# Two-layer hybrid diffusion step on one Trainium2 core: sixteen modulation tiles move from layer 0's value stage to its input stage

## The reference, cut to what matters

```python
m = jax.nn.silu(cvec) @ w_mod + b_mod          # per layer: 6 rows of 1024, for c_ctx and for c
...
hp = adaln(xp, g_norm2[layer], mp[:, 3], mp[:, 4])
xp = xp + mp[:, 5][:, None, :] * peer(hp, peer_wq[layer], peer_subkeys[layer], peer_u[layer], peer_v[layer])
...
# peer, for each block of 128 tokens
q = (xb @ wq).reshape(tb, PEER_HEADS, 2, PEER_DK // 2)
sc = jnp.einsum('thsd,hskd->thsk', q, subkeys)          # 8 heads x 2 x 128 keys
# top 16 of each half, top 16 of their 256 sums: 128 experts of 16384 for each token
act = jax.nn.gelu(jnp.einsum('td,thkd->thk', xb, u_tab[idx]))
out = jnp.einsum('thk,thkd->td', (gsm * act), v_tab[idx])
```

## Time and profile before

| | |
|---|---|
| median of 3 runs | 4231.42 us (4229.95 to 4235.04) |
| profiled execution, its own time | 4233.31 us |
| its span, first to last instruction | 4231.5 us |
| mean granted clock of TensorE | 0.984 |
| busy: PE / DVE / POOL / ACT | 4083.5 / 2841.0 / 2218.1 / 1221.0 us |
| layer 0's input stage, end of its last matmul | 1395.46 us |
| layer 0's value stage, its first matmul | 1397.98 us |

### The profile page before, as it was taken

The page is one execution under the profiler, slowest core; times in us unless marked ns, Lnnn a source line. Parts: engine busy times, 40 slices in busy tenths (PEclk is TensorE's granted clock), DMA queues, the critical chain, the costliest instruction groups (busy, mean ns, idle before and its releaser), DMA issues.

```text
span 4231.5 us, 57020 instructions
## 1 busy us (share of the span) xinstructions
PE 4083.5 (97%) x19676; PEld 3440.7 (81%) x19676; DVE 2841.0 (67%) x5039; ACT 1221.0 (29%) x1744; POOL 2218.1 (52%) x1784
## 2 busy tenths in 40 slices
PE   7988999999999999999898889999999999999998
PEld 6768988888888788888796689888888888888886
DVE  7877896998125897878634448969981116666665
ACT  2332012232322232333233420122322223333332
POOL 3324447777777554445331134477777755444441
PEclk9989999999999999999999999999999999999999
DMA  5743223333345998888514512333333339888883
GB/s 206 274 175 105 66 107 130 127 129 127 129 143 192 362 350 315 313 313 312 184 54 146 219 65 66 107 130 127 127 129 127 129 120 343 294 290 290 290 287 135
DMA packets 336774, 796.94 MB, mean 188 GB/s; under 512 B 71424, under 2 KB 73184, under 8 KB 336128
## 3 DMA queue, kind: packets, MB, share of 16 engines
q1 hardware_dynamic: 175248, 500.38, 33.4%
q10 hardware_dynamic: 83568, 159.94, 10.2%
q0 software_dynamic: 77824, 134.97, 9.7%
HBM read 640.67 MB, written 154.42 MB: 188 GB/s over the span
## 4 chain that ended last, share of the span: by engine, by line
PE 91%; DVE 5%; DMA 1%; ACT 1%; issue 1%; SPq 0%; POOL 0%; DVEq 0%; ACTq 0%; POOLq 0%
PE acc L605 15%; PE acc L607 15%; PE acc L606 15%; PE aux L887 5%; PE acc L889 5%; PE acc L888 5%; PE aux L888 5%; PE acc L887 5%; PE aux L889 5%; PE acc L842 3%; PE acc L844 3%; PE acc L843 3%; PE aux L812 1%; PE aux L770 1%; DVE unread L1472 1%
## 5 line engine op out<-in xcount | busy, mean ns | idle before, releaser
L574 POOL DMA_INDIRECT gate_d<-gate_v,spot_i x1024 | 1140.3, 1114 | 371.1 <-issue 341.8
L605 PE MATMUL acc<-a_hi,w_hi 128*128 128x512 f32 (+1 forms) x3248 | 1182.8, 364 | 35.0 <-DVE a_lo L1445 30.6
L606 PE MATMUL acc<-a_lo,w_hi 128*128 128x512 f32 (+1 forms) x3248 | 1171.2, 361 | 0.0
L607 PE MATMUL acc<-a_hi,w_lo 128*128 128x512 f32 (+1 forms) x3248 | 1171.1, 361 | 0.0
L605 PEld LDWEIGHTS acc<-a_hi,w_hi 128*128 128x128 f32 x3248 | 613.9, 189 | 130.0 <-issue 48.2
L606 PEld LDWEIGHTS acc<-a_lo,w_hi 128*128 128x128 f32 x3248 | 613.8, 189 | 80.9 <-issue 1.0
L607 PEld LDWEIGHTS acc<-a_hi,w_lo 128*128 128x128 f32 x3248 | 613.2, 189 | 80.1
L1680 DVE TENSOR_TENSOR w_lo<-w_in,w_hi 128x1024 fp32r<-128x1024 f32 x224 | 273.1, 1229 | 573.3 <-ACT w_hi L1213 569.9
L541 POOL DMA_INDIRECT found<-in_v,where_i x256 | 321.1, 1254 | 510.6 <-DVE total L1867 415.1
L1846 DVE TENSOR_TENSOR w_lo<-w_in,w_hi 128x1024 fp32r<-128x1024 f32 x256 | 312.8, 1223 | 223.5 <-ACT w_hi L1252 221.4
L522 POOL CAST w_hi<-w_in 128x1024 fp32r<-128x1024 f32 (+1 forms) x89 | 98.9, 1111 | 664.1 <-DMA w_in<-in_wq 228.4
(11 more groups left out here) (275 smaller groups left out, 5991.4 us busy)
## 6 DMA issues: line engine op xcount, KB each, us to landing
w_in<-in_u SPq DMA_DIRECT2D x256, 512.0 KB, 5.1
w_in<-in_v SPq DMA_DIRECT2D x256, 512.0 KB, 4.9
gate_d<-zeros ACTq DMA_DIRECT2D x32, 2048.0 KB, 7.5
act_s<-l_out ACTq DMA_DIRECT2D x256, 256.0 KB
ag<-act_s SPq DMA_DIRECT2D x256, 256.0 KB, 4.8
ag<-gate_d SPq DMA_DIRECT2D x256, 256.0 KB, 5.7
w_in<-in_in SPq DMA_DIRECT2D x32, 512.0 KB, 7.7
w_in<-in_wq SPq DMA_DIRECT2D x32, 512.0 KB, 3.5
```

Source lines behind the costliest of these rows:

```text
L574: pool.indirect_dma_start(gate_d[l], bass.IndirectOffsetOnAxis(ap=spot_i[:, n, k:k + 1], axis=0), gate_v[:, n, k:k + 1], None).then_inc(sp ...
L605: pe.matmul(out, wh, hi[:, k, n], start=(k == 0), stop=False)
L606: pe.matmul(out, wh, lo[:, k, n], start=False, stop=False)
L607: return pe.matmul(out, wl, hi[:, k, n], start=False, stop=(k == kt - 1))
```

## The change

`MODS_U` goes from 16 to 32 and `MODS_AT` from 112 to 88. Layer 0's input stage then has 40 tiles instead of 24, one beside each of the chunks 88 to 127, and none behind them. The value stage has 16 tiles instead of 32, one in each body, in one buffer instead of two: ahead of chunk 6 in the first body, of chunk 4 in the others. SyncE's part of the input stage is written out for 40 chunks instead of 16, with its wait for `shifted` ahead of chunk 88 instead of chunk 112.

```diff
@@ -276,8 +276,8 @@
         block = ctx.enter_context(nc.Block())
 
         N_CONST, N_CONST1 = 10, 5
-        MODS_U = 16
-        MODS_AT = 14 * SPLIT
+        MODS_U = 32
+        MODS_AT = 11 * SPLIT
         MODS_LATE = 8
         MODS_B, MODS_D, MODS_C = range(16, 26), range(26, 32), range(32, 40)
         B_BESIDE, D_BESIDE = (1, 7), (8, 9, 11, 12, 14, 16)
@@ -459,9 +459,8 @@
                         load_modulation(t)
                     for c in range(MODS_AT, NKEY):
                         load_inputs(c // SPLIT, c % SPLIT)
-                        load_modulation(c - MODS_AT + 4)
-                    for t in range(NKEY - MODS_AT + 4, MODS_LATE + MODS_U):
-                        load_modulation(t)
+                        if c - MODS_AT + 4 < MODS_LATE + MODS_U:
+                            load_modulation(c - MODS_AT + 4)
 
                 def load_values(c, u):
                     slot = u
@@ -490,18 +489,17 @@
                     sp.wait_ge(a_st[s], 16 * A_ALL[s] * (l + 1))
                 for u in range(GROUP, SPLIT):
                     load_ag(u, u)
-                    if l == 0 and u < GROUP + 2:
-                        sp.dma_start(w_mod_v[u - GROUP][:], a["w_mod"][1, MODS_U + u - GROUP])\
-                          .then_inc(mod_v_in[u - GROUP], 16)
+                    if l == 0 and u == GROUP:
+                        sp.dma_start(w_mod_v[0][:], a["w_mod"][1, MODS_U]).then_inc(mod_v_in[0], 16)
                 with sp.Fori(1, BODIES) as i:
                     for u in range(SPLIT):
                         load_ag(u + SPLIT * i, u)
                         sp.wait_ge(v_done, NKEY * l - SPLIT + u + 1 + SPLIT * i)
                         load_values(u + SPLIT * i, u)
-                        if l == 0 and u in (0, 4):
-                            sp.wait_ge(mod_v_used, 2 * i + u // 4 - 1)
-                            sp.dma_start(w_mod_v[u // 4][:], a["w_mod"][1, bass.ds(MODS_U + u // 4 + 2 * i, 1)]
-                                         .rearrange("o p n -> (o p) n")).then_inc(mod_v_in[u // 4], 16)
+                        if l == 0 and u == 0:
+                            sp.wait_ge(mod_v_used, i)
+                            sp.dma_start(w_mod_v[0][:], a["w_mod"][1, bass.ds(MODS_U + i, 1)]
+                                         .rearrange("o p n -> (o p) n")).then_inc(mod_v_in[0], 16)
             for k in range(KD):
                 sp.wait_ge(y_ready, k + 1)
                 sp.dma_start(a["y"][:, k, :], y[:, k, :]).then_inc(y_out, 16)
@@ -1802,8 +1800,6 @@
                         modulate_u(c - MODS_AT)
                     low_u(l, c)
                 if l == 0:
-                    for t in range(NKEY - MODS_AT, MODS_LATE + MODS_U):
-                        modulate_u(t)
                     dve.wait_ge(mod_u_used, MODS_LATE + MODS_U)
                     add_bias(0, 40, 48)
                 step(dve.scalar_tensor_tensor(where[:, 0, :], picks[:, 1, 0, :], float(P), picks[:, 0, 0, :],
@@ -1827,17 +1823,16 @@
                     dve.tensor_tensor(p_los[:, k, :], ag[:, k % 4, 0, :], p_his[:, k, :].bitcast(F), ALU.subtract)\
                        .then_inc(p_lo, 1)
 
-                def modulate_v(i, s):
-
-                    dve.wait_ge(mod_v_in[s], 16 + 16 * i)
+                def modulate_v(i):
+
+                    dve.wait_ge(mod_v_in[0], 16 + 16 * i)
                     for c in range(2):
-                        wait(dve, mod_v_sum, 2 * s + c + 4 * i)
-                        dve.tensor_tensor_reduce(out=unread_v[:], in0=w_mod_v[s][:], in1=c_all[:, c, :], scale=1.0,
+                        wait(dve, mod_v_sum, c + 2 * i)
+                        dve.tensor_tensor_reduce(out=unread_v[:], in0=w_mod_v[0][:], in1=c_all[:, c, :], scale=1.0,
                                                  scalar=0.0, op0=ALU.mult, op1=ALU.add,
-                                                 accum_out=mod_v[:, s, c:c + 1]).then_inc(mod_v_sum, 1)
-                    dve.wait_ge(mod_v_sum, 2 * s + 2 + 4 * i)
-                    dve.tensor_copy(mod[:, 1, bass.ds(MODS_U + s + 2 * i, 1), :], mod_v[:, s:s + 1, :])\
-                       .then_inc(mod_v_used, 1)
+                                                 accum_out=mod_v[:, 0, c:c + 1]).then_inc(mod_v_sum, 1)
+                    dve.wait_ge(mod_v_sum, 2 + 2 * i)
+                    dve.tensor_copy(mod[:, 1, bass.ds(MODS_U + i, 1), :], mod_v[:, 0:1, :]).then_inc(mod_v_used, 1)
 
                 def low_v(i, u):
 
@@ -1870,8 +1865,8 @@
                 def chunk(i, u, q=None, half=0, first=False):
 
                     form(i, u)
-                    if l == 0 and u in ((6, 7) if isinstance(i, int) and i == 0 else (3, 7)):
-                        modulate_v(i, 1 if u == 7 else 0)
+                    if l == 0 and u == (6 if isinstance(i, int) and i == 0 else 4):
+                        modulate_v(i)
                     if q is not None:
                         if u % 4 == 0:
                             parts(q, half)
```

## The result

The changed kernel has a median of 4241.8 us (4236.38 to 4248.04, 12 runs) against 4231.94 for the kernel before on the same chips (12 runs). The ratio is 1.0023, 95% interval 1.0015 to 1.0031: slower by 9.9 us, between 6.3 and 13.1. The forecast was 4237.3 with a range of 4228.5 to 4246, and its likeliest class was "within 0.2%"; the result is in the range, and just beyond the 8.5 us that were to part "slower" from "same"; its interval lies on both sides of that line. The profiled execution took 4239.78 us, its span 4238.0.

The account below looks back on a forecast made before the run. TensorE was taken to bound the kernel, with 91% of the chain that ended last. First wait 8.4, clock 2.0 and second wait 0, less 2.52 and 2.02, gave +5.9 us on 4231.42: 4237.3 us, range 4228.5 to 4246.

Parts of the forecast that it names:

- Sixteen tiles out of the value stage: Value stage: 36.50 us of DVE work leaves, all under a full PE, so 0 us gained.
- Eight tiles from the end of the input stage: Seam to the value stage: 18.3 us of DVE work goes, shortening PE's two waits; 3.0 us gained at best.
- Chunks 88 to 127 without a wait of PE: Input stage: 24 more chunks with a tile leave PE without waits; SyncE's wait for shifted has 86 us to spare.
- The scatters: POOL, layer 0's input stage: tiles stretch gate scatters to 1.618 us each; the last ends at about 1393.6, 26.5 us later.
- The price of a tile: POOL's scatters beside DVE's tiles: each tile costs 1.07 us, not all of its 2.28.
- The third rival: Input stage: tiles block POOL for their whole 2.28 us, scatters run to 1421.8, time 4265.5 us; chance 0.02.
- From the last scatter to PE: Seam: landing 2.0, act_s issue 0.5, gate half of ag 5.7, chain to PE 2.1 us; first value matmul at 1403.9.
- The landing of 2.0 us: Seam: the last scatter takes 2.0 us to land before SyncE goes on, within 1.35 to 7.8.
- The clock: Seam: after its 8.4 us wait PE restarts at a lower clock, losing 2.0 us, between 0 and 2.5.
- The second wait: PE at chunk 4 of the value stage: the old wait of 2.02 us for w_lo falls to 0.
- Three marks that were to show a right forecast: Profile after: last scatter issued between 1388 and 1398, first p_los wait 5 to 11 us, no w_lo wait at chunk 4.
- the slower rival: Seam: landing 7.8 and ag 7.5 us beside POOL's row fetches, first value matmul 1411.5, time 4244.9 us; chance 0.28.

Follow-up runs that it names:

- e5: Kernel before with only the changed kernel's value stage, input stage as before, the 16 tiles between left out; 0.9994 of the kernel before.
- e4: Kernel before with its 24 input-stage tiles beside chunks 104 to 127 and none behind, value stage keeping 32 tiles; 0.9993 of the kernel before.
- e9: Changed kernel with each tile's two products replaced by two sums over the weights alone, one input instead of two; 0.9995 of the kernel before.
- e6: Changed kernel with POOL's first eight row fetches of layer 0 issued behind the first eight pick_act; 1.0022 of the kernel before.
- e8: Changed kernel with a third product of 128 x 1024, result unused, in each of the input stage's 40 tiles; 1.0053 of the kernel before.

## Why the prediction was right, and where it was not, point by point

*Sixteen tiles out of the value stage, 0 us:* right, by PE's 655.00 us of 655.00, and in time, by e5, within 0.15%.

*Eight tiles from the end of the input stage, 3.0 us at best:* right at the seam. e4, which takes the eight from the end and nothing from the value stage, has a first wait of 1.51 and no second one. In time it is 0.9993, not told from 1. In the changed kernel the gain isn't there to be had.

*Chunks 88 to 127 without a wait of PE, and SyncE's wait for shifted hidden:* right; PE's waits have no row between 640 us and the seam.

*The scatters:* the mechanism was right, and so was the pitch with tiles, 1.618 us forecast and 163.40/101 = 1.618 measured, 170.6 scatters forecast by 1371.3 and 169 measured. That the pitch agrees to the last digit is luck: POOL stands idle now and then, which the profile puts down to "issue", and the stretch of the earlier trace rows with tiles has 4.21 us of that in it, the first stretch here 3.10, the second none. Counted without, the pitch was 1.56 before and is 1.59 and 1.62 now. What was mis-sized is the rest: 16.4 scatters in 22.3 us forecast, 19 in 30.1 us measured (1371.3 to 1401.38). An idle stretch of 4.44 us, ahead of 1381.30, fell there. It did not fall there by chance: in layer 0 of every trace 128 scatters lie between one such stretch and the next, and where all 512 are there the last stretch stands ahead of the last 15. So the trace of before could have told where it would be. The last scatter came at 1401.4 and not at 1393.6.

*The price of a tile:* 1.07 us was near enough, but the prediction took it for less than a full block. Each hold is a full one, of one scatter by one operation (e9's rows). The third rival, 2.28 us a tile, failed because every second product finds POOL at work on a scatter that has already been held.

*From the last scatter to PE, 10.3 us:* measured 6.88. The landing of 2.0 us was right (SyncE goes on 1.41 us after the last issue, POOL 2.02). The gate half of ag lands within 2.95 us of its issue, not 5.7: little else was under way (DMA share 0.22 from 1400 to 1405), and the median that I took is over all ag loads, most of them in the value stage's busy DMA (0.83). By luck this error, 3.4 us, goes against that of the scatters, 7.8 us: first value matmul at 1408.26 instead of 1403.9, with inputs that ended 1.25 us later, a first wait of 11.55 instead of 8.4.

*The clock, 2.0 us:* from 1408.26 to 1415 PE issued 4 + 19 matmuls where 6.74/0.2262 = 29.8 would have gone at 2.4 GHz: 1.5 us.

*The second wait, 0:* wrong; 2.02 us. The sum let chunk 4 hang on `pick_act` as before. What held it was ag of chunk 4, behind 4 MB of rows and 2 MB of value loads that all start once the scatters have landed (e6). Before, ag of chunks 0 to 3 had gone out from 1384.24 on the earlier trace rows, ahead of both.

Three marks that were to show a right forecast were missed: the last scatter's issue at 1400.43 instead of 1388 to 1398, a first wait of 11.55 us instead of 5 to 11, and the second wait.

By the measured terms the sum is 11.55 + 1.5 + 2.02 - 2.52 - 2.02 = +10.5 us, and the clock showed +9.9 (6.3 to 13.1). The case that came is the likeliest one by its mechanism and the slower rival by its point (first value matmul behind 1406.5); that rival's own reason, a late landing and a slow ag, did not happen at the first chunk, and the slow ag came at chunk 4 only.

## What to carry to other kernels

Work that moves off a busy engine into another stage must be priced on every engine that shares something with it there, not on its own engine's idle time: DVE had room for 24 more tiles, but POOL, which issues the scatters that open the next stage, had 28 us of cover, and they took 34. Where a stage opens on an indirect DMA stream, compute the lead of its last issue over the end of the work that covers it and treat it as a budget. Here some 5.4 us are needed, the 6.9 from the last scatter to PE less the 1.5 that PE waits anyway: nothing is lost at the first wait while the lead lasts, and each microsecond beyond it is lost in full. And when a gate opens late, all that queued behind it starts at once, so a load that is not the first can be late too, as ag of chunk 4 was.

## What was not expected of the hardware

A DVE product of two SBUF tensors beside POOL's scatters stretches a scatter from 0.96 us to as much as 2.0, and a sum over one tensor of the same length leaves the pitch at 1.37 us against 1.36 without tiles. Less expected: the price isn't proportional to DVE's time. A scatter is held until the operation that it starts beside ends, and ends 0.82 to 0.84 us behind it; the next operation in a row falls on those 0.83 us and the 0.30 behind them. So two products in a row held one scatter a tile, and a third one none more (41 scatters in 40 tiles, in the changed kernel and in e8). Traffic of 512 KB loads (DMA share 0.60 against 0.41) did not slow the scatters at all. And POOL's stream of indirect DMAs stood idle for 3.0 to 6.9 us after every 128 scatters in layer 0, in all eleven traces; for what, none of them shows.
